# Eight more z units by Strassen pairs, three plain units a tile, and a loop over two tiles

## The reference, cut to what matters

```
h = rms_norm(x);  proj = h @ w_in  ->  q | k | v | z_attn | z_ssd | xBC | dt | gate_logits
branch A: sliding-window attention(q, k, v) * silu(z_attn), then @ w_attn_proj
branch B: SSD(conv(xBC), dt), rms_norm(y * silu(z_ssd)), then @ w_ssd_proj
out = x + (sigmoid(gate_a) * A + sigmoid(gate_b) * B) @ w_out
```

## Time and profile before

| | |
|---|---|
| median of 3 runs | 1361.34 us |
| the profiled execution | 1362.73 us, of which the span is 1360.9 us |
| granted clock of TensorE | 0.997 of full speed |
| PE busy | 1344.9 us (99%), 7104 matmuls |
| VectorE, ScalarE, GpSimd busy | 58%, 45%, 43% |

### The profile page before, as it was taken

The page is one execution under the profiler, slowest core; times in us unless marked ns, Lnnn a source line. Parts: engine busy times, 40 slices in busy tenths (PEclk is TensorE's granted clock), DMA queues, the critical chain, the costliest instruction groups (busy, mean ns, idle before and its releaser), DMA issues.

```text
span 1360.9 us, 20335 instructions
## 1 busy us (share of the span) xinstructions
PE 1344.9 (99%) x7104; PEld 1078.2 (79%) x7104; DVE 793.5 (58%) x949; ACT 609.0 (45%) x1145; POOL 585.9 (43%) x338
## 2 busy tenths in 40 slices
PE   7999999999999999999999999999999999999999
PEld 6878777888888777878787888878878878788787
DVE  6857777766776364646455555555455544577411
ACT  7564454554455362526353534444456533322200
POOL 3544654454455353424242424242347666444320
PEclk8999999999999999999999999999999999999999
DMA  7433654433323656373737373737555365435331
GB/s 213 179 83 116 165 157 133 147 107 121 108 93 108 211 173 239 121 259 114 265 119 247 121 231 121 231 121 247 210 208 216 117 230 187 160 126 184 138 108 62
DMA packets 123195, 221.14 MB, mean 162 GB/s; under 512 B 7777, under 2 KB 84321, under 8 KB 119826
## 3 DMA queue, kind: packets, MB, share of 16 engines
q1 hardware_dynamic: 58178, 172.12, 37.5%
q10 hardware_dynamic: 64880, 48.37, 11.3%
q0 software_dynamic: 96, 0.13, 0.0%
HBM read 152.05 MB, written 63.31 MB: 158 GB/s over the span
## 4 chain that ended last, share of the span: by engine, by line
PE 87%; DVE 7%; ACT 2%; issue 1%; POOL 1%; DMA 1%; DVEq 0%; ACTq 0%; SPq 0%; POOLq 0%
PE F L196 38%; PE F L1024 29%; PE F L1979 3%; PE M L1979 3%; PE M L1228 2%; PE M L1272 2%; DVE sb_acc L1895 2%; DVE sb_acc L1893 1%; PE F L1266 1%; PE F L1259 1%; PE F L1242 1%; PE M L1266 1%; PE M L1259 1%; DVE sb_acc L1890 1%; ACT sb_X L1827 1%
## 5 line engine op out<-in xcount | busy, mean ns | idle before, releaser
L196 PE MATMUL F<-sb_xb,sb_whl 128*128 128x512 f32 x1536 | 374.3, 400 | 0.0
L196 PEld LDWEIGHTS F<-sb_xb,sb_whl 128*128 128x128 f32 x1536 | 285.5, 188 | 73.8 <-issue 8.1
L208 POOL TENSOR_TENSOR sb_whl<-sb_wst,sb_whl 128x1024 fp32r<-128x1024 f32 x64 | 156.9, 2451 | 363.4 <-ACT sb_whl L205 362.9
L196 PE MATMUL F<-sb_X,sb_whl 128*128 128x512 f32 x1104 | 258.7, 395 | 0.7 <-POOL sb_whl L208 0.7
L196 PEld LDWEIGHTS F<-sb_X,sb_whl 128*128 128x128 f32 x1104 | 206.9, 187 | 52.1 <-issue 1.4
L1024 PE MATMUL F<-sb_tv,sb_whl 128*128 128x512 f32 x1008 | 241.8, 395 | 0.0
L1024 PEld LDWEIGHTS F<-sb_tv,sb_whl 128*128 128x128 f32 x1008 | 188.9, 187 | 46.3
L437 POOL TENSOR_TENSOR sb_whl<-sb_acc,sb_whl 128x512 fp32r<-128x512 f32 x103 | 145.2, 1417 | 134.3 <-ACT sb_whl L494 134.3
L1024 PE MATMUL F<-sb_xb,sb_whl 128*128 128x512 f32 x756 | 184.5, 396 | 0.6 <-POOL sb_whl L437 0.6
L1024 PEld LDWEIGHTS F<-sb_xb,sb_whl 128*128 128x128 f32 x756 | 141.1, 187 | 38.7 <-issue 2.5
L1511 ACT ACTIVATE sb_res<-F 128x512 f32<-128x512 f32 x64 | 38.5, 601 | 228.6 <-PE F L196 228.6
(11 more groups left out here) (225 smaller groups left out, 1778.0 us busy)
## 6 DMA issues: line engine op xcount, KB each, us to landing
sb_wst<-w_units SPq DMA_DIRECT2D x64, 512.0 KB, 4.9
sb_acc<-cs_d SPq DMA_DIRECT2D x8, 2048.0 KB, 8.1
sb_wst<-w_units SPq DMA_DIRECT2D x12, 1024.0 KB, 5.2
x_d<-sb_res ACTq DMA_DIRECT2D x24, 512.0 KB, 3.2
sb_acc<-w_units SPq DMA_DIRECT2D x10, 1024.0 KB, 4.9
sb_early<-x_d SPq DMA_DIRECT2D x8, 1024.0 KB, 6.8
sb_acc<-ecs_d SPq DMA_DIRECT2D x16, 512.0 KB, 7.7
z_d<-sb_res ACTq DMA_DIRECT2D x16, 512.0 KB, 2.6
```

Of the source, the lines that this page charges most:

```text
L196: last = nc.tensor.matmul(bank, weight(slot, wp, k), act(ap, k, half), start=(k == 0 and wp == 0 and ap == 0), stop=(k == NK - 1 and wp == 1))
L208: return nc.gpsimd.tensor_tensor(weights(slot, 1), raw_unit(slot), weights(slot, 0).bitcast(f32), ALU.subtract)
```

## The change

Units 0 to 7 of `z_ssd` become four more pairs at the end of block 1 (25 pairs in all). ScalarE applies Silu to them there and stores them to rows 0 to 7 of `z_d`. A tile of block 2 has three plain units in place of four: one of `z_ssd` (rows 8 to 15) and two of the gate logits. As three is odd and there are two weight slots, the loops of block 2 run over two tiles (3 times), and the last two tiles are written out. In block 3 the first eight z rows are not passed through Silu again. VectorE's order within a tile stays as it was, with the two minima ahead of the second scaling.

```diff
-B2, B3 = 0, 32
+PER_TILE = 3
+B2, B3 = 0, PER_TILE * NT
-         + [("x", X0U + 2 * i) for i in range(12)] + [("z", Z0 + 4), ("z", Z0 + 6)])
+         + [("x", X0U + 2 * i) for i in range(12)] + [("z", Z0 + 4), ("z", Z0 + 6)]
+         + [("z", PLAIN + 4 * i) for i in range(4)])
...
+                if m < 4:
+                    act.dma_start(by_tile(za_d, 2 * m + u), in_tiles(raw[:, u, :])).then_inc(z_stored[u], 16)
+                else:
+                    act.dma_start(z_d[2 * (m - 4) + u], raw[:, u, :]).then_inc(z_stored[u], 16)
...
 (all engines' tile loops)
-            with loop(0, NT - 1) as j:
-                yield j, False
-            yield NT - 1, True
+            with loop(0, NT // 2 - 1) as i:
+                for s in range(2):
+                    yield i, s, i * 2 + s, False
+            yield NT // 2 - 1, 0, NT - 2, False
+            yield NT // 2 - 1, 1, NT - 1, True
...
 (PE)
                 b_rows_and_cb()
-                half_unit(2)
                 attend(0)
                 attend(1)
                 pe.wait_ge(norm_ready, at(4, 4))
                 probs_T(2)
                 probs_T(3)
-                half_unit(3)
+                half_unit(2)
                 attend(2) ... x_rows(3)
-                half_unit(4)
+                half_unit(3)
                 diag(0) ... new_state(1)
-                half_unit(5)
-                half_unit(6)
+                half_unit(4)
                 diag(2) ... new_state(3)
-                half_unit(7)
+                half_unit(5)
...
 (ScalarE)
                 unit_out(0)
                 decay(0)
-                take_half(2)
                 probs_out(2)
                 probs_out(3)
                 decay(1)
-                take_half(3)
+                take_half(2)
                 (last tile: store of the attention output)
+                take_half(3)
                 unit_out(1)
-                take_half(4)
                 decay(2)
                 decay(3)
-                take_half(5)
-                unit_out(2)
+                take_half(4)
                 (last tile: the splits of X1; before, take_half(6) stood ahead of the fourth)
-                take_half(7)
-                unit_out(3)
+                take_half(5)
+                unit_out(2)
...
 (GpSimd)
-                low(pool, B2 + 0 + 2, 4, j)
+                next_low(0)
                 (skip product)
-                low(pool, B2 + 1 + 2, 4, j)
                 x_dd(2), x_dd(3), decay_state(0), decay_state(1)
-                low(pool, B2 + 2 + 2, 4, j)
+                next_low(1)
                 (decay_state(2), decay_state(3); last tile: the lows of X1)
-                low(pool, B2 + 3 + 2, 4, j)
+                next_low(2)
...
 (block 3, ScalarE and VectorE)
-                act.wait_ge(y_in[s], i * 32 + (16 * q0 + 32))
-                nc.scalar.activation(tile(X, 0, i, s), tile(X, 0, i, s), ACT.Silu).then_inc(silu3, 1)
+                if q0:
+                    (the same two lines)
-                dve.wait_ge(silu3, i * 2 + n)
+                if q0: dve.wait_ge(silu3, i * 2 + (s + 1))
+                else:  dve.wait_ge(y_in[s], i * 32 + 32)
```

More of the change, by code:

```diff
@@ L34 @@
 PLAIN, UNITS = 45, 109
[L35 removed]
+PER_TILE = 3
+B2, B3 = 0, PER_TILE * NT
 PAIRS = ([("k", K0), ("z", Z0), ("z", Z0 + 2)] + [("q", Q0 + 2 * i) for i in range(4)]
[L37 removed]
+         + [("x", X0U + 2 * i) for i in range(12)] + [("z", Z0 + 4), ("z", Z0 + 6)]
+         + [("z", PLAIN + 4 * i) for i in range(4)])
+NZ = 8
 NPAIR = len(PAIRS)
@@ L75, in loop, with tiles @@
         self.n = base + count * steps
[L77 to L81, removed]
+    def tiles(self, eng_loop, steps):
+        for i in self.loop(eng_loop, NT // 2 - 1, 2 * steps):
+            for s in range(2):
+                yield i, s, i * 2 + s, False
+        yield NT // 2 - 1, 0, NT - 2, False
+        yield NT // 2 - 1, 1, NT - 1, True
 SCRATCH = "Internal"
@@ L213, in build, with unit_row @@
         p_hi, p_lo, prod = sems("p_hi", "p_lo", "prod")
+        def unit_row(u, c, at):
+            if type(at) is int:
+                u, c, at = at * c + u, 0, 0
+            if u >= B3:
+                return at * c + (PLAIN + NT + u)
+            t, s, n = u // (2 * PER_TILE), u // PER_TILE % 2, u % PER_TILE
+            if n == 0:
+                return at * 4 + (PLAIN + 2 * NT + 4 * t + s)
+            return at * 8 + (PLAIN + 8 * t + 4 * s + 1 + n)
         def load_w(sp, u, c, at):
@@ L219, in load_w @@
                 sp.wait_ge(w_lo, at * c + (u - 1))
-            src = a["w_units"][ds(at * c + (PLAIN + u), 1)] if c else a["w_units"][PLAIN + u:PLAIN + u + 1]
+            src = a["w_units"][ds(unit_row(u, c, at), 1)]
             sp.dma_start(raw_unit(u % 2), src.rearrange("a p c -> (a p) c")).then_inc(w_in[u % 2], 16)
@@ L1157, in load_bc, with tile_loads, next_w @@
                 sp.dma_start(bc[:], x_d[ds(j, 1), :, 16:24, :].rearrange("a p n t -> (a p) n t")).then_inc(bc_in, 16)
-            def tile_loads(j, at_j, first, last_tile=False):
+            def tile_loads(i, s, j, at_j, first, last_tile=False):
+                def next_w(n):
+                    load_w(sp, B2 + PER_TILE * s + n + 2, 2 * PER_TILE, i)
                 sp.wait_ge(sc_done, j * 4 + 1)
@@ L1175, in tile_loads @@
                     load_bc(j, at_j)
-                    load_w(sp, B2 + 2, 4, j)
+                    next_w(0)
                 else:
-                    load_w(sp, B2 + 2, 4, j)
+                    next_w(0)
                     load_decays(j, at_j)
@@ L1183, in tile_loads @@
                     for p in range(2):
-                        sp.wait_ge(z_stored[p], 16 * 4)
+                        sp.wait_ge(z_stored[p], 16 * NZ)
                 sp.dma_start(zo[:], za_d[ds(j, 1)].rearrange("a p n t -> (a p) n t")).then_inc(z_in, 16)
@@ L1189, in tile_loads @@
                                  ecs_d[ds(j, 1), h, :].rearrange("a c -> (a c)").partition_broadcast(HD)).then_inc(ecs_in, 16)
-                for n in range(3, 5):
-                    load_w(sp, B2 + n, 4, j)
+                next_w(1)
                 if last_tile:
@@ L1196, in tile_loads @@
                         sp.dma_start(X1[:, 1, k, :].bitcast(f32), o_d[k]).then_inc(o_in[k], 16)
[L1197 to L1202, removed]
+                next_w(2)
+            tile_loads(0, 0, 0, 0, True)
+            tile_loads(0, 1, 1, P, False)
+            with nc.sync.Fori(1, NT // 2 - 1) as i:
+                for s in range(2):
+                    tile_loads(i, s, i * 2 + s, sp.snap(i * (2 * P) + s * P), False)
+            tile_loads(NT // 2 - 1, 0, NT - 2, (NT - 2) * P, False)
+            tile_loads(NT // 2 - 1, 1, NT - 1, (NT - 1) * P, False, True)
         @block.tensor
@@ L1209, in _ @@
             pe.wait_ge(b12_moved, 32)
-            for j, last_tile in tiles(nc.tensor.Fori):
+            for i, s, j, last_tile in tiles(nc.tensor.Fori):
                 def at(n, k):
@@ L1276, in half_unit @@
                     if h % 2 == 0:
[L1277 to L1280, removed]
+                        pe.wait_ge(w_hi, at(PER_TILE, B2 + n + 1))
+                        pe.wait_ge(w_lo, at(PER_TILE, B2 + n + 1))
+                    pe.wait_ge(half_taken, at(2 * PER_TILE, h + 1))
+                    matmuls(F2[:, h % 2, :], (PER_TILE * s + n) % 2, first_act, h % 2).then_inc(unit_done, 1)
                 pe.wait_ge(q_in, at(16, 16))
@@ L1349, in _ @@
             ch.link(nc.vector.tensor_scalar(stat[:, 5, :], C("sinks"), -1.0, None, ALU.mult))
-            for j, last_tile in ch.loop_and_last(nc.vector.Fori, NT, 4 * 3 + 2 * 2):
+            for i, s, j, last_tile in ch.tiles(nc.vector.Fori, 4 * 3 + 2 * 2):
                 def at(n, k):
@@ L1476, in _ @@
             act.wait_ge(ncs_ready, 1)
-            for j, last_tile in tiles(nc.scalar.Fori):
+            for i, s, j, last_tile in tiles(nc.scalar.Fori):
                 def at(n, k):
@@ L1506, in take_half @@
                 def take_half(h):
-                    n, p = h // 2, (h // 2) % 2
-                    act.wait_ge(unit_done, at(8, 2 * B2 + h + 1))
+                    m = PER_TILE * s + h // 2
+                    p = m % 2
+                    act.wait_ge(unit_done, at(2 * PER_TILE, 2 * B2 + h + 1))
                     if h % 2 == 0:
-                        act.wait_ge(stored[p], at(32, 16 * (n // 2) + BLOCK1_STORES))
+                        act.wait_ge(stored[p], i * (16 * PER_TILE) + (16 * (m // 2) + BLOCK1_STORES))
                     nc.scalar.activation(res[:, p, (h % 2) * HALF:(h % 2 + 1) * HALF], F2[:, h % 2, :], ACT.Copy).then_inc(half_taken, 1)
                 def unit_out(n):
[L1514 to L1517, removed]
+                    m = PER_TILE * s + n
+                    p = m % 2
+                    high(act, B2 + m + 2, 2 * PER_TILE, i)
+                    act.wait_ge(half_taken, at(2 * PER_TILE, 2 * n + 4))
```

(23 more changed lines are left out.)

4 lines of the change are left out of this document (removed).

## The result

The changed kernel takes 1368.71 us (median of 5 runs, 1368.18 to 1369.76) against 1361.6 of the kernel before in the same comparison (5 runs). The ratio is 1.0054, with an interval of 1.0042 to 1.0065: it is slower by 7.1 us, where I had forecast 8.2 faster. The profiled execution has a span of 1368.0, also 7.1 above the 1360.9 of before.

The account below looks back on a forecast made before the run. PE was taken to bound the kernel, busy 1344.9 of 1360.9 us. Terms -90.9 + 78.4 + 3.3 + 1.7 - 0.7 = -8.2 took 1361.34 to 1353.1 us, range 1348.5 to 1358.

Parts of the forecast that it names:

- Bound by PE, and no sum of another engine: Whole kernel and block 2 tile: PE busy 1344.9 of 1360.9 us; only a chain of waits could otherwise bound it.
- Four pairs, +78.4: End of block 1: four added pairs of 84 matmuls, 19.60 us each on PE, add 78.4 us.
- Two halves a tile, -11.36, and the waits that take their place: Block 2: two half units removed save 11.36 us a tile, 90.9 over eight; new waits cost 3.3.
- my 3.3: Block 2: PE's waits for the second scaling, 0.7 us in the first tile and 0.37 in seven others.
- 0.3 and 1.2 us of cover: Block 2 tiles: time left before PE would wait at attend 0 and at the second diagonal; cost taken as 0.
- Entrance of block 3, +1.7 and -0.7: VectorE's low part ahead of y delays PE's first unit 1.7 us; a vanished weight low-part wait gives back 0.7.
- a fixed price of company: Last tile: alternative where VectorE's low part takes 2.96 us beside GpSimd, making the delay 3.0 instead of 1.7.
- Two tiles in a loop: Block 2 loops: same instructions with half as many jumps back, so nothing won or lost.
- Rival C: Block 2: minima ahead of the second scaling collide with GpSimd, 1.6 us a tile; 1366.0 us, chance 0.04.
- The sign of being wrong that I had named: Block 2: the tiles' waits together passing 8 us would show the forecast wrong.

Follow-up runs that it names:

- e3: The changed kernel with PE's tiles written out and VectorE's second scaling moved ahead of the two minima: 1352.34 us, ratio 0.9927.
- e1: The changed kernel with only PE's eight tiles written out, other engines keeping their loops over two tiles: 1354.73 us, ratio 0.9947.
- e4: The kernel before with PE's eight tiles written out instead of looped one tile at a time: 1362.68 us, ratio 1.0002.
- e2: The kernel before with PE's loop alone run three times over two tiles, the last two written out, no work changed: 1380.41 us, ratio 1.013.

## Why the prediction was wrong, by its own steps

*Bound by PE, and no sum of another engine.* Right.

*Four pairs, +78.4.* Right: block 2 begins at 554.79 instead of 476.48, +78.3.

*Two halves a tile, -11.36, and the waits that take their place.* Right as a sum in each undisturbed tile. The first, a middle and the last tile of before last 66.02, 65.20 and 61.37; less 11.36 and plus the wait that is 55.4, 54.2 and 50.4, and the windows show 55.4 (from 554.79), 54.0 to 54.8 and 50.25. That the sum fits so well is in part luck, as its two terms are off by about as much in opposite directions. A tile with no wait for the second scaling lasts 54.03 (the seventh, and tiles 3 to 7 of e3) and not 65.20 - 11.36 = 53.84, so the halves gave 11.17 a tile, 1.5 us less over eight. Most of this is at attend 0: from the eight matmuls of C·B to what follows it is 624.00 - 623.19 = 0.81 where a half unit follows (before), and 626.65 - 625.67 = 0.98 where attend 0 does (the changed kernel). The rows of C·B, before and then in the changed kernel:

```profile
623.19 1.06 PE L1253 MATMUL M<-sb_early 128*128 128x128 f32 x8
```

```profile
625.67 1.06 PE L1278 MATMUL M<-sb_early 128*128 128x128 f32 x8
```

The waits are smaller than I had them. The wait for the second scaling is there, and it is 0.47 in the second tile:

```profile
626.65 1.09 PE L1267 MATMUL F<-sb_early 128*64 128x128 f32 x16
628.22 1.09 PE L1253 MATMUL M<-sb_cst,sb_early 128*128 128x128 f32 x8 [0.47 <-DVE sb_early L1411]
```

PE could have gone on at 626.65 + 1.03 = 627.68. Without the jumps the term is 2.4 us against my 3.3, by the medians of e1 and e3; the first seven tiles of the two (555.16 to 936.08, and 555.23 to 934.03) differ by 2.1. In e1 it was 0.5 in the first tile and not 0.7, 0.5 in the second, 0.2 to 0.35 by their lengths in the next four, and the last two tiles had none. No wait appeared at attend 0 or at the second diagonal, as I had said, with 0.3 and 1.2 us of cover.

*Entrance of block 3, +1.7 and -0.7.* Right, with 1.3 for the 1.7: from the start of that unit to the end of its first half it takes 1009.15 - 1001.83 = 7.32 against 1001.10 - 995.11 = 5.99, so +1.3.

```profile
1001.10 16.96 PE L196 MATMUL F<-sb_X,sb_whl 128*128 128x512 f32 x72
```

```profile
1001.83 4.40 PE L1958 MATMUL F<-sb_X,sb_whl 128*128 128x512 f32 x18
...
1009.15 84.16 PE L201 MATMUL F<-sb_X,sb_whl 128*128 128x512 f32 x360
```

VectorE's low part stood ahead of y as foretold and took 1.62 us, not 1.23 and not 2.96:

```profile
996.47 1.62 DVE L1364 TENSOR_TENSOR sb_X<-sb_X 128x1024 fp32r<-128x1024 f32 x1 [3.47 <-ACT sb_X L1589]
998.01 0.67 DVE L1430 TENSOR_TENSOR sb_acc<-sb_acc,M 128x512 f32<-128x512 f32 x1
```

```profile
994.61 5.75 POOL L1643 TENSOR_TENSOR sb_X<-sb_X 128x1024 fp32r<-128x1024 f32 x2 [7.57 <-ACT sb_X L1589]
```

With 1.23 for VectorE's own work inside GpSimd's 5.75, one of GpSimd's two takes (5.75 - 1.23) / 2 = 2.26 and the first ends at 996.87 (the profile's spans of GpSimd are rough, so this is an estimate). Blocking until then would give 0.4 of wait and 1.2 of work, which is what the row shows. It fits the rule of the Trainium skill, page "SBUF — State Buffer", section "Who interferes with whom", better than a fixed price of company. The 0.72 us wait for a weight's low part is gone.

*"Two tiles in a loop. The same instructions, with half as many jumps back. ... nothing is won or lost."* This is the step that failed: 2 x 7.4 = 14.8 us, where no other term is off by more than 2. I read the cost of a jump back from a body of one tile, where it is nothing (e4 confirms it), and took it to be the same for a body nearly twice as long. The row that I cited, 65.20 of 65.20 busy, could not bound it: no loop in the trace of before had a long body. I counted the jumps, and should have counted what each jump goes over. The sum closes with it: 78.3 for the pairs, 1001.83 - 554.79 = 447.0 against 995.11 - 476.48 = 518.6 for the tiles, so -71.6, +1.3 and -0.7 at the entrance, together +7.3, against 7.1 measured. Rival C had the sign, but its mechanism, minima that collide with GpSimd ahead of the second scaling, did not occur. The sign of being wrong that I had named, waits of the tiles that together pass 8 us, did appear, with 9.6 us of a kind that I had not thought of.

What stays open: why the pause of e2 is longer than that of the changed kernel and in two pieces (the rest of its higher price is the lower clock), what sets a pause's length (the DMA engines were 0.99 busy from 664.99 to 671.51), where between 1344 and 1556 instructions the cost sets in, and whether the other engines' longer bodies cost anything. PE's unrolling brought the kernel to within 1.6 us of the forecast, so there is little left for them.

## What to carry to other kernels

When an edit makes a loop body longer, count the body's instructions on each engine, matmuls and weight loads both, before taking the jump back as free; where PE is the bound, write the turns out rather than jump over a long body. An idle entry with "issue" for its releaser, in the middle of a group of equal instructions and at a loop's head, beside more instruction packets in the page's DMA part, is the sign of it. And on the engine that was never the bound, move work whose result is wanted late behind work that PE waits for: it cost nothing here and gave 2.4 and 1.0 us once the cover was gone.

## What the runs showed of the hardware

A jump of PE back over a body of 1556 matmul and weight-load instructions cost 7.4 us, and 9 packets of 16 KB on the instruction queue; over 1748 it cost 8.2 and 9.5 us, over 672, 874 and 1344 nothing. Behind a pause of 4.7 us the granted clock was 0.50 for 3.5 us and 0.64 for the 3 us after, and this lower clock cost some 3.0 us: about 1.7 in the rest of the scores and 1.3 in the next 48 matmuls.
